# Mixture-of-experts closing body: the last expert's join matmuls moved into its gate/up stage, its last weight piece loaded row by row

## The reference, cut to what matters

```python
D_MODEL = 1024; SEQ = 256; DEC_BATCH = 8; DEC_SEQ = 4      # 256 + 32 = 288 tokens
N_EXPERTS = 32; TOP_K = 4; D_FF = D_MODEL

def expert_block(args):
    xb, e = args
    h = xb @ w_gu[e] + b_gu[e]
    gt = jnp.minimum(h[:, :D_FF], SWIGLU_LIMIT)
    up = jnp.clip(h[:, D_FF:], -SWIGLU_LIMIT, SWIGLU_LIMIT)
    return ((up + 1.0) * (gt * jax.nn.sigmoid(SWIGLU_ALPHA * gt))) @ w_dn[e] + b_dn[e]

    # _moe: y[token] = sum over its 4 experts of gate * expert(x[token])

def _finish(...):
    mix = (jax.nn.sigmoid(ga) * (nsa_o @ w_pa) + jax.nn.sigmoid(gb) * (hg_o @ w_pb)) @ w_o
    h = _layernorm(DN_ALPHA * x + mix, ln1_g, ln1_b)
    return _layernorm(DN_ALPHA * h + _moe(h, *moe_w), ln2_g, ln2_b)
```

## Time and profile before

| | |
|---|---|
| median of 3 runs | 1399.89 us (1399.02 to 1400.67) |
| the profiled execution, its own time | 1398.3 us |
| its span | 1396.6 us |
| granted TensorE clock over the span | 0.996 |
| TensorE busy | 1355.6 us (97%) |
| TensorE weight loads busy | 692.7 us (50%) |
| VectorE busy | 434.5 us (31%) |
| ScalarE busy | 247.6 us (18%) |
| gate/up products of one piece, 16 matmuls | 3.65 us |
| mean transfer rate over the span | 342 GB/s |

### The profile page before, as it was taken

The page is one execution under the profiler, slowest core; times in us unless marked ns, Lnnn a source line. Parts: engine busy times, 40 slices in busy tenths (PEclk is TensorE's granted clock), DMA queues, the critical chain, the costliest instruction groups (busy, mean ns, idle before and its releaser), DMA issues.

```text
span 1396.6 us, 21218 instructions
## 1 busy us (share of the span) xinstructions
PE 1355.6 (97%) x8324; PEld 692.7 (50%) x8324; DVE 434.5 (31%) x940; ACT 247.6 (18%) x448; POOL 92.6 (7%) x122
## 2 busy tenths in 40 slices
PE   9999999999999999999999999999999999999986
PEld 6666999867675533433343334333343333333322
DVE  0345764864336421222122112211121111212114
ACT  1125531352313210111101100110010110011001
POOL 0031400204000000000000000000000000000000
PEclk9999999999999999999999999999999999999998
DMA  8831340738796899999999999999999999999994
GB/s 296 288 107 54 114 167 8 212 121 272 212 347 267 359 393 421 426 427 428 428 428 428 428 429 428 429 429 428 428 428 429 428 429 429 428 428 428 427 428 177
DMA packets 79329, 477.08 MB, mean 342 GB/s; under 512 B 9686, under 2 KB 38054, under 8 KB 54374
## 3 DMA queue, kind: packets, MB, share of 16 engines
q1 hardware_dynamic: 75028, 465.12, 82.4%
q0 software_dynamic: 2288, 9.51, 1.9%
q10 hardware_dynamic: 1954, 1.63, 0.4%
HBM read 471.81 MB, written 8.59 MB: 344 GB/s over the span
## 4 chain that ended last, share of the span: by engine, by line
PE 76%; DMA 21%; DVE 1%; ACT 1%; issue 0%; SPq 0%
PE bank L1395 22%; DMA big<-in_w_gu 20%; PE bank L1452 12%; PE bank L1051 5%; PE bank L1321 4%; PE bank L1333 3%; PE bank L813 3%; PE bank L797 2%; PE bank L1220 2%; PE bank L868 2%; PE bank L870 2%; PE bank L876 2%; PE bank L1238 2%; PE bank L794 1%; PE bank L847 1%; PE bank L751 1%
## 5 line engine op out<-in xcount | busy, mean ns | idle before, releaser
L1452 PE MATMUL bank<-big,gates 128*64 128x512 f32 x768 | 175.4, 599 | 0.0
L1395 PE MATMUL bank<-big,gates 128*64 128x512 f32 x640 | 145.2, 596 | 9.5 <-DMA big<-in_w_gu 9.5
L2587 DVE TENSOR_SCALAR gates<-bank 128x512 f32<-128x512 f32 x32 | 22.1, 691 | 406.8 <-PE bank L1395 406.8
L2612 DVE TENSOR_TENSOR work<-work,bank 128x512 f32<-128x512 f32 x124 | 79.4, 681 | 160.4 <-PE bank L1333 160.4
L1395 PE MATMUL bank<-big,work 128*64 128x512 f32 x512 | 113.4, 595 | 0.0
L1452 PEld LDWEIGHTS bank<-big,gates 128*64 128x64 f32 x768 | 50.9, 136 | 103.9 <-issue 101.2
L1762 ACT ACTIVATE gates<-gates 128x512 f32<-128x512 f32 x32 | 20.2, 630 | 445.7 <-DVE gates L2587 445.7
L1850 POOL TENSOR_TENSOR work<-small,nsaT 128x192 f32<-128x192 f32 x64 | 30.7, 510 | 944.6 <-PE bank L1345 828.5
L1395 PEld LDWEIGHTS bank<-big,gates 128*64 128x64 f32 x640 | 44.6, 137 | 97.0 <-issue 85.2
L1395 PE MATMUL bank<-big,front_cols 128*64 128x512 f32 x384 | 87.4, 597 | 4.4 <-DMA big<-in_w_gu 4.1
L1321 PEld LDWEIGHTS bank<-small,work 128*128 128x128 f32 x512 | 62.3, 192 | 23.1 <-issue 23.1
(11 more groups left out here) (432 smaller groups left out, 1709.3 us busy)
## 6 DMA issues: line engine op xcount, KB each, us to landing
big<-in_w_gu SPq DMA_DIRECT2D x96, 2048.0 KB, 29.9
big<-in_w_dn SPq DMA_DIRECT2D x48, 2048.0 KB, 32.2
front_rows<-in_w_gu SPq DMA_DIRECT2D x16, 2048.0 KB, 29.8
front_cols<-in_w_gu SPq DMA_DIRECT2D x15, 2048.0 KB, 29.5
front_cols<-in_w_dn SPq DMA_DIRECT2D x8, 2048.0 KB, 32.6
front_rows<-in_w_dn SPq DMA_DIRECT2D x8, 2048.0 KB, 33.5
big<-in_w_in SPq DMA_DIRECT2D x5, 2048.0 KB, 8.5
big<-in_cache_cmp_kv SPq DMA_DIRECT2D x64, 128.0 KB, 2.6
```

The source lines that it names most:

```text
L1395: last = pe.matmul(psum[2 + n][half * CAP:(half + 1) * CAP, :], xe[q // 2][k // 4][:, k % 4, of * CAP:(of + 1) * CAP], weights_gu(slot, k ...
L1452: last = pe.matmul(psum[5][half * CAP:(half + 1) * CAP, :], act_T[:, k % 4, (k // 4) * CAP:(k // 4 + 1) * CAP], ring_dn[slot][:, k % 4, ha ...
L2612: dve.tensor_tensor(y, y, psum[6 + half][:, :], ALU.add).then_inc(y_added, 1)
```

## The change

Only the closing body and what serves it are changed. On TensorE, in expert 31: `turn_gates` stands ahead of the first gate/up product, behind a wait for the copy of expert 30's turned gates; `bring_rows(0)` and `join_rows(0)` follow the products of piece 0, `bring_rows(1)` and `join_rows(1)` those of piece 1; tile 2's identity product and join with expert 30 stand between the gate/up stage and the transposes. The banks of tiles 1 and 2 change places. The last down piece is loaded by four transfers of 512 KB, each with a semaphore of its own. On ScalarE `pgT_last` is copied at the start of expert 31. The last joins with expert 31 go tile 0, tile 1, tile 2, and VectorE measures them in that order.

```diff
-LAST_BANKS = [6, 2, 0]
+LAST_BANKS = [6, 0, 2]
...
+END_SLOT = (4 * PIECES - 2) % NSLOT
...
+        end_loaded = [(wout_loaded, 48), (wo_loaded, 64), (x_again, 96), (x_loaded, 32)]
...
-            def load_piece(slot, e, j):
+            def load_piece(slot, e, j, by_rows=False):
...
-                sp.dma_start(dst, src.rearrange("o (p a) n -> (o p) a n", p=P)[:, rows, :]).then_inc(piece_loaded[slot], 16)
+                src = src.rearrange("o (p a) n -> (o p) a n", p=P)
+                if by_rows:
+                    for a in range(4):
+                        sp.dma_start(dst[:, a, :], src[:, a, :]).then_inc(end_loaded[a][0], 16)
+                else:
+                    sp.dma_start(dst, src[:, rows, :]).then_inc(piece_loaded[slot], 16)
...
-                    load_piece((n - 1) % NSLOT, expert_at(e), j)
+                    load_piece((n - 1) % NSLOT, expert_at(e), j, last and n == 4 * PIECES - 1)
...
                 pe.wait_ge(u_ready, i + 1)
+                if final:
+                    pe.wait_ge(pgT_copied, i + 1)
+                    turn_gates(pair, of)
+                    pe.wait_ge(y_added, i * 5 + 5)
...
                     if k % 2:
                         last.then_inc(piece_free, 1)
+                    if final and k == 1:
+                        pe.wait_ge(ye_copied, i + 1)
+                        bring_rows(0)
+                        join_rows(0, pgT, ye, False)
+                    elif final and k == 3:
+                        pe.wait_ge(pgT_copied, i + 2)
+                        bring_rows(1)
+                        join_rows(1, pgT, ye, False)
...
                 if final:
-                    pe.wait_ge(y_added, i * 5 + 5)
-                    bring_rows(0)
-                    join_rows(0, pgT, ye, False)
-                    turn_gates(pair, of)
+                    pe.wait_ge(g_ready, i + 1)
+                    pe.matmul(psum[LAST_BANKS[2]][:, 0:D // 4], ident, y_sum[:, 2, 0:D // 4], start=True, stop=False, skip_group_check=True)
+                    join_rows(2, pgT, ye, False)
...
-                if final:
-                    bring_rows(1)
-                elif more_rows:
+                if more_rows:
                     gather(pair + 1, of, tiles=(1,))
                 pe.wait_ge(act_copied, i + 2)
                 for k in range(KD):
-                    if k % 4 == 0:
+                    if final and k >= 4:
+                        slot = END_SLOT
+                        pe.wait_ge(end_loaded[k - 4][0], end_loaded[k - 4][1] + 16)
+                    elif k % 4 == 0:
                         slot = piece(4 + k // 4)
...
-                if final:
-                    join_rows(1, pgT, ye, False)
-                else:
+                if not final:
...
             last_one = rounds * NE
-            pe.wait_ge(pgT_copied, last_one + 1)
             pe.wait_ge(ye_copied, last_one + 1)
             join_rows(0, pgT_last, ye_last, True)
-            pe.matmul(psum[LAST_BANKS[2]][:, 0:D // 4], ident, y_sum[:, 2, 0:D // 4], start=True, stop=False, skip_group_check=True)
-            join_rows(2, pgT, ye, False)
+            join_rows(1, pgT_last, ye_last, True)
             join_rows(2, pgT_last, ye_last, True)
-            join_rows(1, pgT_last, ye_last, True)
...
+                if final:
+                    take_gates_turned(i, pgT_last)
                 act.wait_ge(g_ready, i + 1)
                 act.wait_ge(act_ready, i + 1)
                 act.activation(sg, g_lim, ACT.Sigmoid, scale=1.702).then_inc(sg_ready, 1)
-                if final:
-                    take_gates_turned(i, pgT_last)
...
             end_stats(0, 0)
             dve.wait_ge(comb_done, last_one * 3 + 2)
+            end_stats(1, 1)
+            dve.wait_ge(comb_done, last_one * 3 + 3)
             q = psum[LAST_BANKS[2]][:, 0:D // 4]
             step(dve.bn_stats(ln_parts[:, 2, 0, :], q))
             dve.bn_aggr(ln_mean[:, 2, :], ln_parts[:, 2, 0:1, :]).then_inc(quarter_ready, 1)
-            dve.wait_ge(comb_done, last_one * 3 + 3)
-            end_stats(1, 1)
```

More of the change, by code:

```diff
@@ L1478, in _ @@
             last_one = rounds * NE
-            pe.wait_ge(pgT_copied, last_one + 1)
             pe.wait_ge(ye_copied, last_one + 1)
             join_rows(0, pgT_last, ye_last, True)
-            pe.matmul(psum[LAST_BANKS[2]][:, 0:D // 4], ident, y_sum[:, 2, 0:D // 4], start=True, stop=False, skip_group_check=True)
-            join_rows(2, pgT, ye, False)
+            join_rows(1, pgT_last, ye_last, True)
             join_rows(2, pgT_last, ye_last, True)
-            join_rows(1, pgT_last, ye_last, True)
             pe.wait_ge(quarter_ready, 4)
-            pe.matmul(psum[1][:, 0:2], mean_of, ln_mean[:, 2, :], start=True, stop=True).then_inc(quarter_done, 1)
+            pe.matmul(psum[3][:, 0:2], mean_of, ln_mean[:, 2, :], start=True, stop=True).then_inc(quarter_done, 1)
             pe.wait_ge(quarter_ready, 5)
-            pe.matmul(psum[1][:, 8:9], mean_of, ln_sum[:, 3:4], start=True, stop=True).then_inc(quarter_done, 1)
+            pe.matmul(psum[3][:, 8:9], mean_of, ln_sum[:, 3:4], start=True, stop=True).then_inc(quarter_done, 1)
         @block.scalar
@@ L2664, in _ @@
             dve.wait_ge(quarter_done, 2)
-            step(dve.tensor_copy(ln_sum[:, 0:2], psum[1][:, 0:2]))
+            step(dve.tensor_copy(ln_sum[:, 0:2], psum[3][:, 0:2]))
             step(dve.tensor_tensor(ln_sum[:, 2:3], ln_mean[:, 2, 0:1], ln_sum[:, 0:1], ALU.subtract))
@@ L2669, in _ @@
             dve.wait_ge(quarter_done, 3)
-            dve.tensor_scalar(ln_rstd[:, 2:3], psum[1][:, 8:9], ln_sum[:, 1:2], LN_EPS, ALU.add, ALU.add).then_inc(ln_var, 1)
+            dve.tensor_scalar(ln_rstd[:, 2:3], psum[3][:, 8:9], ln_sum[:, 1:2], LN_EPS, ALU.add, ALU.add).then_inc(ln_var, 1)
             end_scale(1, 1)
```

## The result

| | before | changed |
|---|---|---|
| median of 15 runs | 1399.93 us | 1402.63 us |
| lowest and highest | 1398.64, 1401.36 | 1401.27, 1404.12 |
| span of the profiled execution | 1396.6 us | 1399.9 us |
| granted TensorE clock | 0.996 | 0.996 |

The ratio of the changed kernel to the one before is 1.0017, with a 95% interval of 1.0011 to 1.0024. The change costs 2.7 us by the medians, 2.4 us by the ratio. The interval lies above 1, so the change is slower; 0.17% is just under the 0.2% that was taken as the edge of what can be told.

A forecast was written before the change was run, and what follows sets the result against it. TensorE bounds expert 31 from piece 3 on. Down starts 3.49 us later, less 0.19 behind it and 0.37 of VectorE standing: +2.9 us on 1399.89, 1402.8 us, 0.21% slower; range 1400.8 to 1404.6 us.

The forecast's parts named there:

- The start's wait: Start of expert 31: TensorE stands 0.68 us for ScalarE's copy of the gates before its first transposes.
- The gate/up stage: Expert 31: four product blocks, two bring-and-join pairs and the biases sum to 21.39 us; its end moves 5.77 us later.
- The room: Expert 31's gate/up stage: two waits for `in_w_gu`, 1.22 and 0.20 us, are all the room, 1.42 us.
- The cover: Gate/up end to down stage, expert 31: expert 30's 3.38 us replaces 5.66 us of work, a gain of 2.28 us.
- The end's order: Behind expert 31's down stage: VectorE measures without the 0.37 us that it stood for tile 1.
- The row-wise load: Last down piece: three more SP issues of 0.33 us, 1 us in all, cost nothing behind 5.3 us of lead.
- the prediction's estimate for smaller transfers: Last down piece: by the skill's page 6.1 us instead of 4.9, 1.2 us off the lead; the sum stays.
- Rival A: Expert 31's gate/up stage: TensorE is not full and the joins fit; end 2.8 us earlier, 1397.1; chance 0.06.
- Rival B: Expert 31: some standing is overlapped or joins cost stream time; +1.4 to +2.7 us, say 1402.0; chance 0.41.
- Rival C: Expert 31's down stage: gaps drop TensorE's clock from 2.4 to 1.2 GHz, adding 7 us, 1409.8; chance 0.03.
- the split at 0.2%: Whole kernel's time: chances of 0.53 for slower, 0.41 for no measurable change, 0.06 for faster; 0.2% is the measurable edge.

## Why the prediction was right

The time, 1402.63 us, is 0.2 us from the 1402.8 forecast. The mechanism is the one that was forecast: work that lay where the activation needed the time anyway was paid in full where TensorE had 1.4 us of room. Step by step, with the changed kernel's times moved back by the 0.38 us that its mark lies later:

| step | forecast | measured |
|---|---|---|
| first gate/up product of expert 31 | 1350.96 | 1350.98 |
| end of the gate/up stage | 1372.35 | 1372.29 |
| waits on the activation | "about 0.7" each (its own terms give 1.86 - 1.27 = 0.59, and 0.77) | 0.60, 0.77 |
| first down product | 1375.73 | 1375.68 |
| start of the down stage to the join behind the bare copy | 7.02 + 0.77 = 7.79 | 7.78, with a wait of 0.70 |
| VectorE starts to measure | 1384.6 | 1384.64 |
| end | +2.93 | +2.91 |

**The start's wait** was priced at 0.68 us; the trace has 0.67, and the run without it gives 0.70 back. **The gate/up stage** took 1372.67 - 1351.36 = 21.31 us, 0.08 less than the sum, in the biases (1369.09 less 1368.06, their first product's start, is 1.03 us, not 1.11). **The room** of 1.42 us was read off two brackets, and four added products measured it as 1.56 us. **The cover** of the activation was taken from expert 30, where it already lay half bare; that it carries over to expert 31 (1376.06 - 1372.67 = 3.39 us against the 3.38 read in expert 30) is the step that did most for the sum. **The end's order** was priced at -0.37 us; in the change VectorE takes 1396.12 - 1385.02 = 11.10 us from tile 0 to its last write against 1392.83 - 1381.29 = 11.54 before, so it gave -0.44 us. **The row-wise load** was priced at nothing and made 0.01 us. The 1.2 us of lead that the prediction's estimate for smaller transfers took off did not show either (36.2 us to landing against 36.6 us).

Rival A, that the joins fit, is refuted by the run with four products more; the share of 50% for weight loads, its ground, says nothing of gaps here. Rival B had the smaller loss come from the gates' copy reaching TensorE sooner or the joins costing only their stream time (1.72 and 0.86 us). Neither happened: the start's wait is 0.67 us, and bring and join take 1.92 and 1.06 us. Rival C, the clock, did not come: the windows of the changed kernel keep a granted clock of 1.00, the 2.4 GHz level, over the down stage and three of the new waits (the fourth, at the start, lies in the window from 1349.8 us to 1363 us, also at 1.00). The Trainium skill (TensorE: Matmul & The Clock Gate, "The HAM clock gate") has the clock fall after idle time; waits of up to 0.77 us were no such time here.

```profile
1363.00:1376.00 13.00, 11.69 (x64) 3.65 (x62) 2.68 (x4) 1.22 (x2) 0.00 (x0) 1.00 0.90 342
1376.00:1384.00 8.00, 7.25 (x34) 2.37 (x36) 0.00 (x0) 0.80 (x3) 0.00 (x0) 1.00 0.02 6
```

Where the prediction was less good is the split at 0.2%. It gave 0.53 to a loss above that and 0.41 to one below, with a forecast of 0.21%; the measured loss is 0.17% by the ratio, and its interval covers both sides. The 0.2 us between forecast and median are within the runs' spread, and by the ratio the loss is 2.4 us, 0.5 less than forecast: what the traces confirm is the 2.93 us of the tail (2.91), while so close a hit on the median is partly luck, and the side of that line was left to chance. One number of its working was loose: SP was to need 1 us more for the four issues and needed 4 us more.

## What to carry to other kernels

Before moving work into an earlier stage, add up the waits in that stage. Here that sum, 1.42 us, was nearly all the room it had (1.56 us by measure), each wait was room only where it stood, and what exceeded it was paid in full. Work that lies between two dependent steps of another engine is partly free: here 5.66 us of it stood where 3.39 us pass without it, so taking it away gave 2.27 us back for the 5.71 us by which the gate/up stage ends later. A neighbouring stage that lacks the filler can show this beforehand, as expert 30 did with 3.38 us. Measured doses, about one product behind each piece, together with the end's order and room made one expert earlier, gave 0.16% where the whole of the change cost 0.17%.

## What the runs showed of the hardware

Splitting one 2 MB load into four of 512 KB, each with 4 KB per partition instead of 16 KB, made SP's issues take 4.36 us together, where one took 0.33 us; one of the four alone took 3.04 us. The issues behind them got slower too: the four small ones of the norm's scale took 8.10 us instead of 1.81 us. Two other kernels with the split show the same: 4.84 and 4.95 us for the four issues, 8.14 and 8.26 us for the ones behind. All of it was hidden: the tail was 46.42 us with the split and 46.41 without. No other split was tried, so whether the packets' number or the queue's fill is behind it stays open.

Pieces do not arrive at the same distance in every execution. At the same place the wait for piece 3 was 0.20, 0.20 and 0.21 us in three profiles and 1.55 us in a fourth, though the windows up to 1350 us show the same 428 GB/s before and in that fourth. In another execution piece 2 came 0.55 us later behind SP's issue than before. Both delays reached the end in full, so a difference of tails below some 1.5 us between two single executions says something only where no piece is waited for, or where the rows show which wait makes it.
